# Stick-breaking attention stage: 1 - beta kept in SBUF, logits two rows ahead, and the transposed blocks split before the row work

## The reference, cut to what matters

```python
def _stick_breaking_attention(q, k, v):
    """A[t,s] = beta_ts * prod_{s<j<t}(1 - beta_tj), s < t only."""
    for i in range(S // Q_BLOCK):                      # 8 blocks of 128 queries
        q0, end = i * Q_BLOCK, (i + 1) * Q_BLOCK
        z = einsum('bthd,bshd->bhts', q[:, q0:end], k[:, :end]) * scale
        causal = s_pos < t_pos
        log_1m_beta = where(causal, log_sigmoid(-z), 0.0)
        tail = cumsum(log_1m_beta, axis=3, reverse=True) - log_1m_beta
        A = where(causal, exp(log_sigmoid(z) + tail), 0.0)
        outs.append(einsum('bhts,bshd->bthd', A, v[:, :end]))
```

## Time and profile before

| what | value |
|---|---|
| median of 3 runs | 1741.71 us (1732.44 to 1743.12) |
| the profiled execution | 1732.67 us, of which its span, first to last instruction, is 1731.0 us |
| PE busy | 1465.2 us, 85% of the span |
| PEld busy | 1203.0 us, 70% |
| DVE busy | 891.7 us, 52% |
| ACT busy | 605.0 us, 35% |
| POOL busy | 557.5 us, 32% |
| mean granted TensorE clock | 0.913 of full speed |

### The profile page before, as it was taken

One profiled execution on the slowest core, in us unless ns is written; L12 is line 12 of the kernel. 1 busy time (PEld: TensorE's weight loads), 2 busy tenths in 40 slices (PEclk: granted clock), 3 DMA queues, 4 the chain that ended last, 5 costly groups with the idle time before them and its releaser, 6 DMA issues. The chain is left out here.

```text
span 1731.0 us, 20506 instructions
## 1 busy us (share of the span) xinstructions
PE 1465.2 (85%) x6865; PEld 1203.0 (70%) x6865; DVE 891.7 (52%) x1567; ACT 605.0 (35%) x1066; POOL 557.5 (32%) x424
## 2 busy tenths in 40 slices
PE   1589998955777678896499499999999999999996
PEld 1466877744666577784387488888888888888884
DVE  5407688894777568886832623323313313313326
ACT  4325666525777546664211521021021011111102
POOL 1143344462443279931400231121121222222214
PEclk9799899987888779897599699999999999999998
DMA  7150233336442065512300411111111111210102
GB/s 292 34 122 13 73 112 131 121 118 144 98 96 51 20 234 189 179 59 92 115 1 0 134 49 48 48 48 48 48 48 48 48 48 37 60 48 25 48 0 97
DMA packets 107278, 139.73 MB, mean 81 GB/s; under 512 B 5704, under 2 KB 79514, under 8 KB 107231
## 3 DMA queue, kind: packets, MB, share of 16 engines
q1 hardware_dynamic: 107232, 139.18, 26.1%
HBM read 114.77 MB, written 20.99 MB: 78 GB/s over the span
## 5 line engine op out<-in xcount | busy, mean ns | idle before, releaser
L1755 DVE TENSOR_TENSOR act_full<-silu_gate,ps_up 128x512 f32<-128x512 f32 x44 | 30.2, 687 | 387.6 <-ACT silu_gate L1614 387.6
L1668 POOL TENSOR_TENSOR wgu_lo<-wgu_raw,wgu_hi 128x2048 fp32r<-128x2048 f32 x22 | 101.4, 4611 | 231.9 <-ACT wgu_hi L1609 231.9
L1768 DVE TENSOR_TENSOR x<-ps_down,x 128x512 f32<-128x512 f32 x176 | 120.0, 689 | 97.0 <-PE ps_down L1728 97.0
L1672 POOL TENSOR_TENSOR wd_lo<-wd_raw,wd_hi 128x2048 fp32r<-128x2048 f32 x11 | 50.6, 4601 | 325.9 <-ACT wd_hi L1619 325.9
L1728 PE MATMUL ps_down<-wd_hi,act_hi 128*128 128x512 f32 x352 | 139.8, 397 | 2.7 <-DVE x L1768 2.7
L1728 PE MATMUL ps_down<-wd_lo,act_hi 128*128 128x512 f32 x352 | 139.4, 396 | 0.0
L1728 PE MATMUL ps_down<-wd_hi,act_lo 128*128 128x512 f32 x352 | 139.3, 396 | 0.0
L1614 ACT ACTIVATE silu_gate<-ps_gate 128x512 f32<-128x512 f32 x44 | 26.4, 599 | 319.5 <-PE ps_up L1716 319.4
L1716 PE MATMUL ps_gate<-h2T_hi,wgu_hi 128*128 128x512 f32 x352 | 137.3, 390 | 0.0
L1716 PE MATMUL ps_gate<-h2T_hi,wgu_lo 128*128 128x512 f32 x352 | 137.1, 389 | 0.0
L1716 PE MATMUL ps_up<-h2T_hi,wgu_lo 128*128 128x512 f32 x352 | 137.0, 389 | 0.0
(11 more groups left out here) (250 smaller groups left out, 3551.0 us busy)
## 6 DMA issues: line engine op xcount, KB each, us to landing
wmod_b<-in_w_mod_dram SPq DMA_DIRECT2D x8, 1536.0 KB, 7.0
wgu_raw<-in_w_gate_dram SPq DMA_DIRECT2D x22, 512.0 KB, 3.9
wgu_raw<-in_w_up_dram SPq DMA_DIRECT2D x22, 512.0 KB, 5.2
wd_raw<-in_w_down_dram SPq DMA_DIRECT2D x11, 1024.0 KB, 4.9
win_raw<-in_w_in_dram SPq DMA_DIRECT2D x20, 512.0 KB, 4.4
wm<-in_w_mod_dram SPq DMA_DIRECT2D x4, 2048.0 KB, 11.4
scr_qkv<-proj_hi SPq DMA_DIRECT2D x16, 512.0 KB, 2.6
scr_qkv<-proj_lo SPq DMA_DIRECT2D x16, 512.0 KB, 3.0
```

The costliest lines, as they stand in the source:

```text
L1668: pool.tensor_tensor(wl[:, m], wr[:, m], wh[:, m].bitcast(F32), ALU.subtract).then_inc(wlr, 1)
L1672: pool.tensor_tensor(dl[:], dr[:], dh[:].bitcast(F32), ALU.subtract).then_inc(dlr, 1)
L1755: dve.tensor_tensor(af[:, u % 2], sg[:, u % 2], ps_u[:, u % 2], ALU.mult).then_inc(gat, 1)
L1768: dve.tensor_tensor(g.x1[:, i, half(c)], ps_d[:, n % 4], g.x1[:, i, half(c)], ALU.add).then_inc(add, 1)
```

## The change

It has four parts.

- ACT writes 1 - beta into a new SBUF tile `one_minus_beta` (two buffers) instead of over z, and writes it before beta. The scan reads it from there. The scan's zero operand, a tile of 1024 columns before, is now one column read by broadcast.
- The `ps_z` buffer is therefore free once beta is written, and PE's wait in `logits` is for `btr` (beta) instead of `scd` (scan). PE issues the logits two rows ahead, `logits(r + 2)` in step r, instead of one.
- In each step ACT does `a_hi` first and then both sigmoids of row r + 1 (before: the sigmoids of row r, then `a_hi`).
- In each step DVE does `a_lo` first and then the scan of row r (before: the scan, then `a_lo`). POOL gets a wait of its own for beta.

```diff
@@ phase2: tiles
         bt = sbuf(nc, ctx, "beta", [P, NB, SEQ])
+        om = sbuf(nc, ctx, "one_minus_beta", [P, NPB, SEQ])
         pb = sbuf(nc, ctx, "stick_left", [P, NPB, WIDE + 1])
-        zero = sbuf(nc, ctx, "scan_zero", [P, SEQ])
+        zero = sbuf(nc, ctx, "scan_zero", [P, 1])
@@ ScalarE
+                def sigmoids(r):
+                    w = P * (rows[r][1] + 1)
+                    act.wait_ge(z_rdy, r + 1)
+                    if r >= NPB:
+                        act.wait_ge(scd, r - NPB + 1)
+                    act.activation(om[:, r % NPB, 0:w], z[:, r % 2, 0:w], ACT.Sigmoid, scale=-1.0).then_inc(omr, 1)
+                    if r >= NB:
+                        act.wait_ge(mul, r - NB + 1)
+                    act.activation(bt[:, r % NB, 0:w], z[:, r % 2, 0:w], ACT.Sigmoid).then_inc(btr, 1)
+
+                sigmoids(0)
                 for r in range(len(of_step)):
-                    if r < NR:
-                        w = P * (rows[r][1] + 1)
-                        act.wait_ge(z_rdy, r + 1)
-                        if r >= NB:
-                            act.wait_ge(mul, r - NB + 1)
-                        act.activation(bt[:, r % NB, 0:w], z[:, r % 2, 0:w], ACT.Sigmoid).then_inc(btr, 1)
-                        act.wait_ge(btr, r + 1)
-                        act.activation(z[:, r % 2, 0:w], z[:, r % 2, 0:w], ACT.Sigmoid, scale=-1.0).then_inc(omr, 1)
...
                         act.activation(ah[:, n % NA, s], tr[:, slot["u", n] % 2, s], ACT.Copy).then_inc(ahr, 1)
+                    if r + 1 < NR:
+                        sigmoids(r + 1)
@@ GpSimd
+                    pool.wait_ge(btr, r + 1)
                     pool.wait_ge(scd, r + 1)
@@ VectorE
                 for r in range(len(of_step)):
+                    for n in of_step[r]:
+                        s = slice(left(n), HALF)
+                        dve.wait_ge(ahr, n + 1)
+                        dve.tensor_tensor(al[:, n % NA, s], tr[:, slot["u", n] % 2, s], ah[:, n % NA, s].bitcast(F32),
+                                          ALU.subtract).then_inc(alr, 1)
                     if r < NR:
                         w = P * (rows[r][1] + 1)
                         dve.wait_ge(omr, r + 1)
                         if r >= NPB:
                             dve.wait_ge(mul, r - NPB + 1)
-                        dve.tensor_tensor_scan(pb[:, r % NPB, WIDE - w:WIDE][:, ::-1], z[:, r % 2, 0:w][:, ::-1],
-                                               zero[:, 0:w], 1.0, ALU.mult, ALU.add).then_inc(scd, 1)
-                    for n in of_step[r]:
-                        s = slice(left(n), HALF)
-                        dve.wait_ge(ahr, n + 1)
-                        dve.tensor_tensor(al[:, n % NA, s], tr[:, slot["u", n] % 2, s], ah[:, n % NA, s].bitcast(F32),
-                                          ALU.subtract).then_inc(alr, 1)
+                        dve.tensor_tensor_scan(pb[:, r % NPB, WIDE - w:WIDE][:, ::-1], om[:, r % NPB, 0:w][:, ::-1],
+                                               zero[:].to_broadcast([P, w]), 1.0, ALU.mult, ALU.add).then_inc(scd, 1)
@@ TensorE
                     if r >= 2:
-                        pe.wait_ge(scd, r - 1)
+                        pe.wait_ge(btr, r - 1)
...
                 logits(0)
+                logits(1)
                 for r in range(len(of_step)):
-                    if r + 1 < NR:
-                        logits(r + 1)
+                    if r + 2 < NR:
+                        logits(r + 2)
```

More of the change, by code:

```diff
@@ L849, in _ @@
                 act.preload_act_table_set("sigmoid_and_others")
-                for r in range(len(of_step)):
-                    if r < NR:
-                        w = P * (rows[r][1] + 1)
-                        act.wait_ge(z_rdy, r + 1)
-                        if r >= NB:
-                            act.wait_ge(mul, r - NB + 1)
-                        act.activation(bt[:, r % NB, 0:w], z[:, r % 2, 0:w], ACT.Sigmoid).then_inc(btr, 1)
-                        act.wait_ge(btr, r + 1)
-                        act.activation(z[:, r % 2, 0:w], z[:, r % 2, 0:w], ACT.Sigmoid, scale=-1.0).then_inc(omr, 1)
[L859 to L867, removed]
@@ new lines, in _ @@
+                sigmoids(0)
+                for r in range(len(of_step)):
+                    if r < NR and r % NT == VSTEP:
+                        h = r // NT
+                        for x in range(2):
+                            act.wait_ge(v_tr, 2 * h + x + 1)
+                            if h >= 2:
+                                act.wait_ge(vd, done_by[2 * h - 3])
+                            act.activation(vs[:, h % 2, 4 * x:4 * x + 4, :],
+                                           tr[:, slot["v", 2 * h + x] % 2].rearrange("p (b d) -> p b d", b=4),
+                                           ACT.Copy).then_inc(v_rdy, 1)
```

## The result

| | before | changed |
|---|---|---|
| median | 1742.1 us (4 runs, 1732.4 to 1743.1) | 1796.5 us (4 runs, 1793.8 to 1801.1) |
| profiled execution, its span | 1732.7, 1731.0 us | 1793.8, 1792.1 us |
| mean granted TensorE clock | 0.913 | 0.902 |

The changed kernel is slower: the ratio is 1.0345, 95% interval 1.0318 to 1.0371, 54 us between the medians and 61 us between the profiled executions. The stage of the stick-breaking heads now ends at 660 us of the span instead of 601. The forecast was 1781 us, with a range of 1756 to 1812.

What follows compares the result with a forecast made beforehand. It took a one-row loop of ACT's `a_hi` and sigmoids, PE's logits and transposes as the bound: 28.0 us per head at full clock plus 2.5 for clock, 6.6 more than before, times 7.4 heads: 49 us, so 1781 us, range 1756 to 1812.

Steps and rivals of the forecast that it cites:

- some 90 or more: Sign in the list of waits: ACT's `a_hi` wait for the transposes grows from 51.9 us and becomes its largest.
- the prediction's own terms for this step: On the one-row loop, per head at full clock: logits 5.8 us, first unit's transposes 4.0, hand-offs 0.8.
- the 28 to 31 that were to show it: Sign: the distance in us from one scan of 256 columns to the next head's.
- 0 where POOL is idle: Extra DVE time for scans reading 1 - beta from SBUF: taken as 0, bounds 0 to 2.8 us per head.
- only the scan of row(0) meets the product of row(7): DVE scan against POOL row product: the loop's only meeting, in a wait that is there anyway.
- the prediction's own price: Half clock on 9.8 us of PE work on the loop: 0.6 x 0.42 added, 2.5 us per head.
- In steps 0 to 4 ACT has no `a_hi` and I count no change: Start of the stage: these steps were taken to keep their length.
- 7.4 heads: Steps 5 to 63, 59 steps with both a row and units; times 6.6 us per head gave 49 us.
- The clock stays at 2.4 GHz: Rival on PE's clock: idle is spread, 28.0 us per head, 30 us more in all, 1763 us; chance 0.18.
- the full-clock sum: Head at full clock: ACT 15.3, logits 5.8, transposes 4.0, hand-offs 0.8, place 2 0.3, turn 1.8; 28.0 us.
- The rival on the faster side: Waits of 41.9 (PE for scan) and 40.5 us (scan for 1 - beta) vanish unreplaced; halfway 1710 us; chance 0.08.
- The product of the turn: Row product of 2.00 us at the head's turn, counted in a 5.5 us chain from `a_hi(7)` to `a_hi(1)`.

Runs made afterwards that it cites:

- e1: The changed kernel with PE making each step's transposes first and then the logits two rows ahead; 1763.6 us, 1.0145 of the kernel before.
- e2: The changed kernel with the logits one row ahead instead of two, still waiting for beta; 1763.5 us, 1.0147 of the kernel before.
- e6: The changed kernel with filler products of a zero tile with v on PE, result unchanged; 1788.1 us, 1.0295 of the kernel before.
- c1: The kernel before with GpSimd's row product cut to the first 128 columns of each row, a control for time alone; 1736.0 us, ratio 0.9977.
- e3: The kernel before with 1 - beta in SBUF before beta and logits waiting for beta, one row ahead, ACT's and DVE's orders unchanged; 1744.1 us, ratio 1.0019.

## Why the prediction was right, and where it was off

One reading of the rows was left half done. Of the two scans of the earlier trace rows the slow one, of 384 columns, ran beside GpSimd, as the kernel before shows; at the one of 640 columns, from 356.04 us, GpSimd was idle.

```profile
344.13 4.22 POOL L544 TENSOR_TENSOR win_lo<-win_raw,win_hi 128x256 fp32r<-128x256 f32 x4 [6.49 <-ACT win_hi L435]
...
344.52 1.31 DVE L761 TENSOR_TENSOR_SCAN cum<-eq 128x384 f32<-128x384 f32 x1
```

- **The direction and the loop.** Right. PE's logits wait for beta, stand in front of the transposes, and ACT's wait for these is 90.4 us ("some 90 or more"). It isn't ACT's largest wait alone, it is the stage's loop: e1 and e2 break it in two ways and give back 4.6 us per head. The step from place 4 to place 5 is 3.74 us in the trace: 0.43 from the start of `a_hi` to that of the sigmoids, 1.52 of sigmoids, 1.09 of logits, 0.60 of transposes and 0.10 of two hand-offs. The last three are the prediction's own terms for this step.
- **The size.** 31.8 us per head against 30.5 (and against the 28 to 31 that were to show it), and 61 us between the profiled executions, 54 between the medians, against 49. The term that was mis-sized is "0 where POOL is idle" for the scan from SBUF, with the claim that "only the scan of row(0) meets the product of row(7)". The scan of row(7) meets the product of row(6), since only a short `a_lo` lies between the two scans: 0.56 us on average, on the turn's chain. That a price of this kind exists was in the earlier trace rows, as said above. The rest of the 1.3 is in part the clock, at half speed for 48% of a head where 42% was taken (0.4 us by the prediction's own price), and in part open.
- **The first head.** "In steps 0 to 4 ACT has no `a_hi` and I count no change", and 7.4 heads. By that count the first head, read as here, grows by about half of what the others do, 4 us. It grew from 20.4 to 26.6 us, by 6.2. It has the wide rows' steps and a whole turn. The last head, from its scan of 256 columns to the end of the stage, grew by only 4.8 us (35.5 to 40.3), so that 7.4 x 7.9 = 58 us comes close to the 59 by which the stage's end moved. That the count fits in sum is luck.
- **The clock.** Its direction was right (0.86 to 0.76). The rival "The clock stays at 2.4 GHz", with its 28.0 us per head, did not come, and with 0.95 in e6 a head was 30.6, not near 28. Of these 2.6 us 0.8 are in the scan of 1024 columns (3119 ns in e6 against 2290), and the filler's delays explain a part; the rest stays open, and with it whether the full-clock sum was too low by more than the collision.
- **The rival on the faster side.** Its two waits did vanish or shrink, as the change meant them to, and the one that took their place was larger. Its second obstacle, that scan and row product exclude each other, is real: with the loop broken (e2) the scans are still 3.2 us per head longer, as much as the head is longer than before. The loop is the larger of the two, 4.6 us per head. Even without both an estimate gives 23.9 us, so nothing here shows that the rival would have come.
- **What no step had seen.** The product of the turn was taken as part of the chain in both kernels; in the kernel before it is nearly hidden (c1).

## What to carry to other kernels

When a wait is moved to an earlier producer, look at what stands between that producer and the next thing its own engine waits for: here beta(r) was the instruction right in front of `a_hi(r)`, and going further ahead with the logits put them in series with ScalarE. Issue on the in-order engine first what another engine waits for now, and then what is for later; that alone was worth 33 of the 54 us here. And before an operand is moved from PSUM to SBUF, look whether GpSimd reads SBUF at the same time: for a scan that then has both operands in SBUF this was a wait for the rest of the GpSimd instruction.

## What the runs showed of the hardware

- A scan with both operands in SBUF that starts while GpSimd multiplies two SBUF tiles takes longer by the rest of that product, less about 0.14 us (in e2 1.18 for 1.31 and 0.94 for 1.08, in the changed kernel 0.27 for 0.41). Where the scan started 0.04 us ahead of the product (e2, 128 columns, at 501.98), it kept its 0.41 us and the product took 2.16 us instead of 2.00. With 1 - beta in PSUM the scan of 128 columns takes 0.41 us inside such a product; in e3, with both in SBUF, 1963 ns on average. Without overlap a scan from SBUF takes as long as one from PSUM: 1.48 and 1.49 us for 640 columns.
- The zero operand as one column read by broadcast costs nothing that shows: 1.48 us for 640 columns, against 1.49 with a whole tile of zeros and 1 - beta in PSUM.
- Fifteen products of 512 columns with a zero tile, put into idle time before each turn, held TensorE at 2.4 GHz through heads two to seven, where it had been at 1.2 GHz for 28% of the time, and made the kernel 0.45% faster.
